# Coarser first pieces and other starting columns for some weight slots in a two-model fp32 kernel

## Reference

```python
def rmsnorm(x, g):
    y = x * lax.rsqrt(jnp.mean(x * x, axis=-1, keepdims=True) + EPS)
    return y * g
def swiglu(x, w_gate, w_up, w_down):
    return (silu(x @ w_gate) * (x @ w_up)) @ w_down

h = x
for l in range(2):
    h = h + 0.5 * swiglu(rmsnorm(h, ffn1_norm[l]), ...)   # D_FF = 2816
    z = rmsnorm(h, mix_norm[l]) @ w_in[l]
    ...                                                   # mixers, gates, w_out
    h = h + 0.5 * swiglu(rmsnorm(h, ffn2_norm[l]), ...)
return second_block(rmsnorm(h, final_norm), ...)
```

## Time and profile before

| | |
|---|---|
| median of 3 runs | 1469.96 us (1467.68 to 1470.48) |
| profiled execution, its own time | 1470.48 us |
| its span, first to last instruction | 1468.7 us |
| PE busy | 1458.0 us (99% of the span) |
| DVE, ACT, POOL busy | 1044.1, 789.1, 39.4 us (71%, 54%, 3%) |
| mean granted TensorE clock | 0.997 |

### The profile page before, as it was taken

One profiled execution on the slowest core, in us unless ns is written; L12 is line 12 of the kernel. 1 busy time (PEld: TensorE's weight loads), 2 busy tenths in 40 slices (PEclk: granted clock), 3 DMA queues, 4 the chain that ended last, 5 costly groups with the idle time before them and its releaser, 6 DMA issues.

```text
span 1468.7 us, 26807 instructions
## 1 busy us (share of the span) xinstructions
PE 1458.0 (99%) x11602; PEld 1377.4 (94%) x11602; DVE 1044.1 (71%) x1440; ACT 789.1 (54%) x1001; POOL 39.4 (3%) x41
## 2 busy tenths in 40 slices
PE   9999999999999999999999999999999999999999
PEld 9999998888999999999999878899999998989978
DVE  7766676787876655766558678777887699666844
ACT  6444455565454444544445566555545645775653
POOL 0000010210000000000001110000000000000000
PEclk9999999999999999999999999999999999999999
DMA  8655545444455555455544444465545453335431
GB/s 332 219 197 186 191 155 198 146 167 148 172 210 188 189 198 201 181 192 201 195 171 186 163 154 150 166 233 201 201 175 199 153 193 133 127 105 195 178 140 58
DMA packets 38837, 262.44 MB, mean 179 GB/s; under 512 B 4672, under 2 KB 5056, under 8 KB 8896
## 3 DMA queue, kind: packets, MB, share of 16 engines
q1 hardware_dynamic: 38576, 260.72, 49.0%
q10 hardware_dynamic: 144, 0.00, 0.0%
HBM read 259.66 MB, written 1.05 MB: 178 GB/s over the span
## 4 chain that ended last, share of the span: by engine, by line
PE 91%; DVE 7%; ACT 1%; issue 1%; DMA 0%; SPq 0%; ACTq 0%
PE ps L243 28%; PE ps L244 28%; PE ps L245 28%; DVE w_low L228 3%; PE ps L1486 1%; DVE scratch L2182 1%; PE ps L1477 0%; DMA w_raw<-in_weights 0%; PE ps L1459 0%; ACT w_high L222 0%; PE ps L1501 0%; DVE even_s_rot L2184 0%; PE ps L2764 0%; PE ps L2779 0%; PE ps L2776 0%
## 5 line engine op out<-in xcount | busy, mean ns | idle before, releaser
L228 DVE TENSOR_TENSOR w_low<-w_raw,w_high 128x2048 fp32r<-128x2048 f32 (+1 forms) x243 | 549.7, 2263 | 234.1 <-ACT w_high L222 233.9
L222 ACT ACTIVATE w_high<-w_raw 128x2048 fp32r<-128x2048 f32 (+1 forms) x243 | 460.1, 1895 | 445.5 <-PE ps L245 443.2
L243 PE MATMUL ps<-x,w_high 128*128 128x256 f32 x1864 | 520.3, 279 | 0.7 <-DVE x L333 0.5
L245 PE MATMUL ps<-x,w_low 128*128 128x256 f32 x1864 | 516.3, 277 | 0.0
L244 PE MATMUL ps<-x,w_high 128*128 128x256 f32 x1864 | 516.3, 277 | 0.0
L243 PEld LDWEIGHTS ps<-x,w_high 128*128 128x128 f32 x1864 | 350.4, 188 | 3.6 <-issue 1.8
L244 PEld LDWEIGHTS ps<-x,w_high 128*128 128x128 f32 x1864 | 350.6, 188 | 0.8 <-issue 0.5
L245 PEld LDWEIGHTS ps<-x,w_low 128*128 128x128 f32 x1864 | 350.7, 188 | 0.0
L243 PE MATMUL ps<-w_high,x 128*128 128x512 f32 (+1 forms) x448 | 165.7, 370 | 0.0
L245 PE MATMUL ps<-w_high,x 128*128 128x512 f32 (+1 forms) x448 | 161.0, 359 | 0.0
L244 PE MATMUL ps<-w_low,x 128*128 128x512 f32 (+1 forms) x448 | 160.7, 359 | 0.0
(11 more groups left out here) (469 smaller groups left out, 2023.1 us busy)
## 6 DMA issues: line engine op xcount, KB each, us to landing
w_raw<-in_weights SPq DMA_DIRECT2D x231, 1024.0 KB, 4.8
w_raw<-in_weights SPq DMA_DIRECT2D x10, 768.0 KB, 4.4
w_raw<-in_weights SPq DMA_DIRECT2D x5, 512.0 KB, 4.1
setup_first<-in_first SPq DMA_DIRECT2D x8, 256.0 KB, 4.7
even_second_vectors<-in_second SPq DMA_DIRECT2D x1, 1836.0 KB, 8.3
resid<-in_x SPq DMA_DIRECT2D x1, 1024.0 KB, 10.1
out<-resid SPq DMA_DIRECT2D x3, 256.0 KB, 2.5
table<-in_table SPq DMA_DIRECT2D x1, 737.0 KB, 8.9
```

The source lines that it names most:

```text
L222: act.activation(self.slot(self.wh, n), self.slot(self.raw, n), ACT.Copy).then_inc(self.hi_made, 1)
L228: dve.tensor_tensor(self.slot(self.wl, n), self.slot(self.raw, n), self.slot(self.wh, n).bitcast(F32), ALU.subtract).then_inc(self.lo_made, 1)
L243: pe.matmul(out, ah, bh, start=start, stop=False, skip_group_check=True)
L245: return pe.matmul(out, al, bh, start=False, stop=stop, skip_group_check=True)
```

## The change

- The eight first DMAs become five: K tiles 0 and 1 by themselves, then three pairs (512 KB, 4 KB in a row of a partition). ACT and DVE treat a pair as one piece: two instructions for x, one of 512 columns for the weights, and PE is told once for a pair.
- Slot 1 is split in two halves of 1024 columns instead of four parts of 512. ACT makes one 128x512 square before each half, the other two after them, and then the high part of slot 2 whole.
- Slot 2 is split whole (128x2048) on DVE too, and this and the sums for the norm move behind the point at which DVE waits for the end of slot 0, sums after slot 2's low part.
- The entries at column 0 move: in the first feed-forward from slot 3 to slot 2; in the others from the third slot to the second (68, 101, 168; 190, 193 and 196 stay); in the mixers from S_UQ (37, 137) to S_CKV (34, 134). The old ones go to column 24.

```diff
-PIECES = DT
-SLOT_PARTS = (PIECES, 4, 2)
+FIRST_TILES = ((0, 1), (1, 2), (2, 4), (4, 6), (6, 8))
+PIECES = len(FIRST_TILES)
...
-MIX_ENTRIES, EVEN_ENTRIES = (S_UQ, S_OUT), (A_GLU,)
+MIX_ENTRIES, EVEN_ENTRIES = (S_CKV, S_OUT), (A_GLU,)
...
-FIRST_AT, APART_AT, LAST_AT = ffn_at((3,)), ffn_at((2,)), ffn_at((2, *TABLE_SLOTS))
+FIRST_AT, APART_AT, LAST_AT = ffn_at((2,)), ffn_at((1,)), ffn_at((1, *TABLE_SLOTS))
...
     def made(self, n):
-        return sum(SLOT_PARTS[:n + 1]) + max(n + 1 - len(SLOT_PARTS), 0)
+        return n + PIECES + (n > 0)
...
 def first_parts(c, pe, n, k):
-    parts = SLOT_PARTS[n]
-    if n == 0:
-        pe.wait_ge(c.xl_made, k + 1)
-    if k % (DT // parts) == 0:
-        pe.wait_ge(c.lo_made, sum(SLOT_PARTS[:n]) + k * parts // DT + 1)
+    for b, (first, _) in enumerate(FIRST_TILES if n == 0 else ()):
+        if k == first:
+            pe.wait_ge(c.xl_made, b + 1)
+            pe.wait_ge(c.lo_made, b + 1)
+    if n == 1 and k % 4 == 0:
+        pe.wait_ge(c.lo_made, PIECES + 1 + k // 4)
...
             dve.wait_ge(*self.filled(2 * s + 1))
+            if late:
+                c.split_low(dve, 2)
+                self.norm.add(dve)
             if s == 0:
                 c.split_low(dve, base + RING)
...
     def high(self, act, b):
         act.wait_ge(*self.arrived(b))
-        act.activation(c.xh[:, b, :], self.rows[:, b, :], ACT.Copy, scale=self.norm.gain[:, b:b + 1]).then_inc(c.xh_made, 1)
+        for k in range(*FIRST_TILES[b]):
+            ins = act.activation(c.xh[:, k, :], self.rows[:, k, :], ACT.Copy, scale=self.norm.gain[:, k:k + 1])
+        ins.then_inc(c.xh_made, 1)
...
     def sync(self, sp):
-        for b in range(PIECES):
-            sp.dma_start(self.room[:, b], self.first[:, b]).then_inc(self.piece_in[b], 16)
+        for b, (first, end) in enumerate(FIRST_TILES):
+            sp.dma_start(self.room[:, first:end], self.first[:, first:end]).then_inc(self.piece_in[b], 16)
...
     def first_scalar(self, act):
         for b in range(PIECES):
             self.high(act, b)
-            self.high_part(act, 0, b)
-        for b in range(SLOT_PARTS[1]):
-            if b % 2 == 0:
-                act.wait_ge((self.half_in, c.landed[1])[b // 2], 16)
-            self.high_part(act, 1, b)
-        for p in range(4):
-            self.norm.square(act, p)
-        act.wait_ge(c.landed[2], 16)
-        for b in range(SLOT_PARTS[2]):
-            self.high_part(act, 2, b)
+            act.activation(self.piece(c.wh, b), self.weight_piece(b), ACT.Copy).then_inc(c.hi_made, 1)
+        for b, s in enumerate((self.half_in, c.landed[1])):
+            self.norm.square(act, b)
+            act.wait_ge(s, 16)
+            act.activation(self.half(c.wh, b), self.half(c.raw, b), ACT.Copy).then_inc(c.hi_made, 1)
+        self.norm.square(act, 2)
+        self.norm.square(act, 3)
+        c.split_high(act, 2)
...
     def first_vector(self, dve):
         for b in range(PIECES):
             self.low(dve, b)
-            self.low_part(dve, 0, b)
-        for b in range(SLOT_PARTS[1]):
-            self.low_part(dve, 1, b)
-        self.norm.add(dve)
-        for b in range(SLOT_PARTS[2]):
-            self.low_part(dve, 2, b)
+            dve.wait_ge(c.hi_made, b + 1)
+            dve.tensor_tensor(self.piece(c.wl, b), self.weight_piece(b), self.piece(c.wh, b).bitcast(F32),
+                              ALU.subtract).then_inc(c.lo_made, 1)
+        for b in range(2):
+            dve.wait_ge(c.hi_made, PIECES + 1 + b)
+            dve.tensor_tensor(self.half(c.wl, b), self.half(c.raw, b), self.half(c.wh, b).bitcast(F32),
+                              ALU.subtract).then_inc(c.lo_made, 1)
```

More of the change, by code:

```diff
@@ L260, in project @@
     xh, xl = x or (c.xh, c.xl)
-    if n >= len(SLOT_PARTS):
+    if n > 1:
         pe.wait_ge(c.lo_made, c.made(n))
     for k in range(kt):
-        if n < len(SLOT_PARTS):
+        if n <= 1:
             first_parts(c, pe, n, k)
@@ L312, in __init__ @@
         self.turned = None if tokens is None else Tally(c.column_made, tokens)
-        self.x_high, self.x_low = (Tally(s, 4 * (i - 1) + PIECES) for s in (c.xh_made, c.xl_made))
+        self.x_high, self.x_low = Tally(c.xh_made, 4 * i + 1), Tally(c.xl_made, 4 * i + 1)
         self.squared = Tally(c.sq_made, 4 * i)
@@ L816, in arrived, with piece, weight_piece @@
         return self.piece_in[b], 16 if b else 32
[L818 to L831, removed]
+    def piece(self, t, b):
+        return self.c.slot(t, 0).rearrange("p (k n) -> p k n", k=DT)[:, slice(*FIRST_TILES[b]), :]
+    def weight_piece(self, b):
+        return self.weights[:, slice(*FIRST_TILES[b]), :]
     def high(self, act, b):
@@ L840, in low, with half @@
         dve.wait_ge(c.xh_made, b + 1)
-        dve.scalar_tensor_tensor(out=c.xl[:, b, :], in0=self.rows[:, b, :], scalar=self.norm.gain[:, b:b + 1],
-                                 in1=c.xh[:, b, :].bitcast(F32), op0=ALU.mult, op1=ALU.subtract).then_inc(c.xl_made, 1)
+        for k in range(*FIRST_TILES[b]):
+            ins = dve.scalar_tensor_tensor(out=c.xl[:, k, :], in0=self.rows[:, k, :], scalar=self.norm.gain[:, k:k + 1],
+                                           in1=c.xh[:, k, :].bitcast(F32), op0=ALU.mult, op1=ALU.subtract)
+        ins.then_inc(c.xl_made, 1)
+    def half(self, t, b):
+        return self.c.slot(t, 1)[:, b * SLOT // 2:(b + 1) * SLOT // 2]
     def sync(self, sp):
         c = self.c
-        for b in range(PIECES):
-            sp.dma_start(self.room[:, b], self.first[:, b]).then_inc(self.piece_in[b], 16)
+        for b, (first, end) in enumerate(FIRST_TILES):
+            sp.dma_start(self.room[:, first:end], self.first[:, first:end]).then_inc(self.piece_in[b], 16)
         for b, s in enumerate((self.half_in, c.landed[1])):
-            half = slice(b * SLOT // 2, (b + 1) * SLOT // 2)
-            sp.dma_start(c.slot(c.raw, 1)[:, half], c.weights[1][:, half]).then_inc(s, 16)
+            sp.dma_start(self.half(c.raw, b), c.weights[1][:, b * SLOT // 2:(b + 1) * SLOT // 2]).then_inc(s, 16)
         for n in range(2, EARLY_SLOTS):
@@ L2932, in model_kernel @@
         even = Even(c, e, DEPTH * LAYER_SLOTS, DEPTH * LAYER_UNITS, norms[-2], norms[-1])
-        odd = Odd(c, o, e.vec, DEPTH * LAYER_SLOTS + EVEN_SLOTS, norms[-1], out, setup.piece_in[1:5])
+        odd = Odd(c, o, e.vec, DEPTH * LAYER_SLOTS + EVEN_SLOTS, norms[-1], out, setup.piece_in[1:])
         with nc.Block() as block:
```

## The result

The median is 1488.26 us (1486.40 to 1492.77, four runs) against 1470.18 for the kernel before, a ratio of 1.0132 with a 95% interval of 1.0105 to 1.0157: 18 us slower, outside the range of the prediction. The profiled execution took 1485.79 us, with a span of 1484.0, 15.3 more than the one before.

What follows compares the result with a forecast made beforehand. The prediction took PE, busy for 1458.0 of 1468.7 us, as the bound. Front end +1.1 and entries -1.2 summed to -0.1 us, giving 1469.9 us against the median of 1469.96, with a range of 1467.2 to 1477.0.

Steps and rivals of the forecast that it cites:

- Entries moved: Column-0 entries in feed-forwards and mixers: starting them earlier shortens slow-pace stretches of PE, -1.2 us together.
- The entry comes too early, and the slow pace lasts: Feed-forward slots after the norm's matmuls: column 24 doesn't cure the pace, 0.20 us a slot, 1494.8 for all stages; chance 0.19.
- The front end: First DMAs to slot 1's start: coarser pieces delay slot 1 from 12.29 to 13.35, costing 1.06 us, say 1.1.
- landing of the first pair: Transfer of K tiles 2 and 3 at the start: there at 6.45 us, bounds 5.6 and 6.9.
- PE's wait before K tile 2: Slot 0, at about 7.8 us: PE idle some 1.1 us until the first pair is handed over.
- The entry moved to slot 2: First feed-forward: slot 2 goes from slow to column 0, slot 3 from column 0 to fast; -0.20 us.
- The rival that SP and the DMA were the bound: Front end: pairs land as soon as ACT is free, costing 0.2 instead of 1.1 us, total 1469.0; chance 0.10.
- The mixers: Entries moved from slots 37 and 137: -0.46 and -0.26, together -0.72 us if slots 35 to 37 stay fast, else about 0.
- Columns don't matter: All moved entries: starting columns don't matter or the new ones bring nothing, leaving +1.1 us alone, 1471.1; chance 0.16.
- The store from slot 193 to 202: Slow stretch of ten slots, worth 2 us if PE comes to it another way, total 1467.0; chance 0.08.

Runs made afterwards that it cites:

- run 5: The changed kernel with the norm's matmuls before K tile 7 instead of 4 in slots 34, 68, 101, 134 and 168; 1477.69 us, ratio 1.0042.
- run 12: The kernel before with only the mixers' entries moved, from slots 37 and 137 to 34 and 134; 1469.77 us, ratio 0.9998.
- run 1: The kernel before with only the entries at column 0 moved as in the change, front end untouched; 1488.03 us against 1469.70, ratio 1.0126.
- runs 3 and 5: The former: the changed kernel with the norm's matmuls before K tile 5 instead of 4 in slots 34, 68, 101, 134, 168; 1473.03 us, ratio 1.0032.

## Why the prediction was wrong

**The step that failed** is in "Entries moved": for the three later feed-forwards "after, the norm's slot at column 0 in both halves (0.16), the next fast: -0.10 each, -0.30". Measured: +6.7, +6.7 and +4.35. The entry is no cure as such; in these stages it works if PE steps off it on a place of the pattern other than the 120. I saw the steps' three averages and not their order. The 14 traces hold 95 exits from column 0 to column 24 in feed-forwards. By the steps in the slot at column 0, and the pace behind it (an ordinary table, from the start times):

| steps in the slot at column 0 | last step | slow behind | fast behind |
|---|---|---|---|
| 120, 113, 116, 118 | 120 | 21 | 0 |
| 120, 113, 116, 118 | 113 to 116 | 0 | 42 |
| 117, 117, 116 | 116 or 117 | 0 | 14 |
| none under 115, mean 118 | 115 or 116 | 13 | 0 |
| none under 115, mean 118 | 119 or 120 | 0 | 2 |
| too few to tell (run 5) | 115 or 116 | 0 | 3 |

So the rule holds without exception where the slot shows the period of four, and is turned round where it shows the steps of the fourth and fifth rows, the slow pace at column 0. Most of these are slots 190, 193 and 196, which begin with four transposes. What leads to one pattern or another is not known. The reader could have found it in the trace of before: slots 196 and 69 are both entries, the one steps off on 120 to slow, the other on 114 to fast.

**The rival "The entry comes too early, and the slow pace lasts"** was the right one: PE comes out of the norm's matmuls into a pace that the step to column 24 doesn't cure. Its price for all stages was 23.2 us. What it lacked is the place in the period, on which this hangs. Measured 17.7: the first stage escaped (6.3 less), and the slots were counted well otherwise (31 x 0.20 = 6.3 against 6.7; by the starts in both traces a slot takes 5.44 or 5.65 us, 0.21 apart). It failed in its chance, 0.19, and in the range. I put the upper end at one stage with a lasting slow pace, 1477, as if the stages were independent throws. They run the same code in the same order behind the same kind of norm, and came out alike: three of three.

**The front end** was right: 1.06 expected, 1.20 measured at slot 1 and 1.10 at slot 4; landing of the first pair 6.45 expected, 6.60 measured; slot 1 at 13.35 and 13.49; slot 2 at 19.1 and 19.24. PE's wait before K tile 2 was 1.59 instead of 1.1, and behind it PE ran slot 0 at the slow pace without another wait, to 13.49. That had hardly an effect: DVE's low part of slot 1's first half ended at 13.41 (12.18 + 1.23), so slot 1 couldn't have begun much earlier. The entry moved to slot 2 gave back 0.1 instead of 0.20: slot 3 lost the 0.16 of column 0, but slot 2, from start to start, got 0.07 longer. The median of the front end alone is 1.7 above that of the kernel before, interval -0.1 to 3.2. The rival that SP and the DMA were the bound is refuted: the first pair landed at 6.60, not at 5.6, and ACT did not wait for slot 1's transfer (11.10 follows its square at 10.58).

**The mixers**: -0.72 expected, +0.3 and 0.0 in the table (between slots 4 and 68, and 134 and 168), 0 in run 12. Slot 35 was slow in the changed kernel, and PE stepped off slot 34 on a 120 here as well; in the first mixer slots 36 and 37 stayed slow too.

**"Columns don't matter"** is refuted by run 1: columns alone make 18 us. By the Trainium skill, "SBUF — State Buffer", section "SBUF: two separate sides", PE's accesses never wait on anyone. Two kernels here that differ in nothing but the starting column of some weights are 18 us apart, so either that sentence doesn't hold for PE's own two streams, weights and moving data, or the cause lies elsewhere in PE; no run here tells which.

**The store from slot 193 to 202** was real (1.0 us in the profiled execution), but not tied to the change: run 1 has the same columns and was slow there.

## What to carry to other kernels

When PE is never idle, look at the distance between the starts of its matmuls, slot by slot: 4% lay there with PE's busy share at 99% in both kernels. A fix that works by where a pattern happens to be when something ends has to be tested where it is to stand, and its failure will be the same in every repeat of the code, so price it for all repeats at once (here three stages out of three). Moving such a fix earlier to save 0.1 us a stage risked 6.7.

## What the runs showed of the hardware

- The same stream of 256-column matmuls with a weight load each runs at 0.1133 or 0.1178 us a matmul (5.44 and 5.65 us for 48), both at the 2.4 GHz level, and stays at either for 170 us or more. Small float32 matmuls in between (the norm's), or a wait (1.59 us before K tile 2), can switch it; a change of the weights' starting column can switch it back.
- At column 0 the steps mostly repeat 120, 113, 116, 118 ns. A step to column 24 after the 120 then gave the slow pace (21 of 21), after a 113 to 116 the fast one (42 of 42); from the two other patterns the table above has what followed. Why is not settled, nor why single executions of runs 3 and 5 are up to 10 us above their lowest.
- The granted clock fell to the 1.2 GHz level around 1243 us in the profiled execution of the kernel before. PE had been busy for 1.08 of the 3 us ahead of it, waiting for DVE (L2345, 2.2 us). The changed kernel waits the same 2.2 us there and kept its clock in its profiled execution. The fall costs 3.2 us. Eight of the 14 profiled executions have it near there, all at a mean granted clock of 0.996 to 0.998; the six without it have 0.999 or 1.000. Before that stretch, of the kernel before (busy us of PE, PEld, DVE, ACT, POOL, then PEclk, DMA share, GB/s):

```profile
1239.00:1242.00 3.00, 1.08 (x10) 0.88 (x8) 2.89 (x7) 1.85 (x10) 0.00 (x0) 1.00 0.42 178
1242.00:1250.00 8.00, 7.67 (x67) 6.95 (x68) 7.83 (x12) 1.76 (x1) 0.00 (x0) 0.57 0.39 141
```
